# Compressing keys and values with two positions stacked over 128 partitions

## The chip, the cores and the metric

The kernel runs on one core of a Trainium2 chip. The metric is the device time of one execution in microseconds (us). Every time below is either a measured run or comes from one profiled execution.

## The reference

The network is two blocks of two layers each over one sequence of 512 tokens with 1024 channels, in float32. The change touches one step in each of the two layers (l = 0 and 1) of the second block: the compression of keys and values ahead of the sparse attention. Cut to that:

```
CMP_BLOCK = 32; CMP_STRIDE = 16          # two heads (Hkv), hd = 64, T = 512, so 31 blocks

def compress_blocks(k, pe, w1, b1, w2):
    B, T, Hkv, hd = k.shape
    n_cmp = (T - CMP_BLOCK) // CMP_STRIDE + 1
    idx = np.arange(n_cmp)[:, None] * CMP_STRIDE + np.arange(CMP_BLOCK)[None, :]
    blocks = k[:, idx] + pe[None, None, :, None, :]
    flat = jnp.transpose(blocks, (0, 1, 3, 2, 4)).reshape(B, n_cmp, Hkv, CMP_BLOCK * hd)
    return jax.nn.gelu(flat @ w1 + b1, approximate=True) @ w2

    kc = compress_blocks(k_cmp, ck_pe, ck_w1, ck_b1, ck_w2)     # k_cmp = rope(kv[:, :, 0])
    vc = compress_blocks(v_cmp, cv_pe, cv_w1, cv_b1, cv_w2)     # v_cmp = kv[:, :, 1]
    s = jnp.einsum('bthgd,bnhd->bhgtn', qg, kc) * scale         # then softmax, selection, o_cmp
```

A block of 32 positions is two neighbouring groups of 16, so the kernel computes each group's product with both halves of `w1` once and adds shifted columns afterwards.

## The kernel before

Each engine has its own program, written out by hand in order, and waits on semaphores. Activations lie as 128 channels by 512 tokens. TensorE (`tensor_program`) works through projections tile by tile; each tile of eight 128x128 weight pieces is three float32r products per piece (lines 546, 549, 553: high by high, low weights, low activations), 512 columns each. ScalarE makes the high part of each weight piece (`hi_to`, line 1111), VectorE the low part (`lo_to`, line 1562), and both start from a raw copy in `ring`.

SyncE (`sync_program`) issues all weight loads, one unit of up to 512 KB at a time (line 503), into a ring of four slots: unit u waits until unit u - 4 has been used. Between the loads, at unit numbers named in `turns`, it issues the half turns of the rotary embedding (`half_turn`, line 481): four transfers of 32 partitions each within SBUF, which move the rotated halves of piece r into `pp`. Pieces r = 0 (the compressed keys), 1 to 4, 5 and 6 wait for VectorE's scaled projection (`ra`). SyncE's queue is in order, so a transfer waits for all that stand ahead of it. GpSimd multiplies the unturned half (line 2319), VectorE the turned one (2076), and VectorE adds them (2081).

In a layer of the second block TensorE does, in this order: a group of five tiles and the tiles 5, 6 and 7 of `w_in` (the last of them is the last work ahead of compression); the compression (line 976); the projection `tm` by token (lines 623 to 627, 280 columns), with the second small product of compression (`compressed`, lines 990 and 995) hooked in after its fourth piece; the compressed scores (1010); eight tiles `sb`; then attention.

The compression at 976 keeps head 0 in partitions 0 to 63 and head 1 in 64 to 127 of `KC` (keys) and `VCB` (values), each with two groups of 16 columns of position embeddings at the ends. For keys, then values, it runs over two units of `w1` (raw, 1024 columns: 16 positions by 64), and for each position over the two heads: 128 products per layer, each with 64 rows of weights, 64 columns and 32 moving columns. The sum lies in two banks. ScalarE copies the keys' bank (1446), converts three `tm` pieces (1111), and applies the gelu (1451) after VectorE's adds (2105 to 2108); the values' bank follows.

## Time and profile before

| | us |
|---|---|
| three runs, median | 2937.4 |
| lowest and highest | 2935.91 and 2937.46 |
| the profiled execution | 2937.69 |
| its span (first to last instruction) | 2936.0 |

| engine | busy us | share of the span |
|---|---|---|
| TensorE, products (PE) | 2919.7 | 99% |
| TensorE, weight loads (PEld) | 2392.5 | 81% |
| VectorE (DVE) | 1821.4 | 62% |
| ScalarE (ACT) | 1305.0 | 44% |
| GpSimd (POOL) | 155.2 | 5% |

### The profile page before, as it was taken

What the parts mean: (1) busy time and instruction counts of PE and PEld (TensorE: products, weight loads), DVE (VectorE), ACT (ScalarE), POOL (GpSimd) and SP (SyncE); (2) the same over time, 40 slices, a digit from 0 to 9 for tenths busy, and PEclk for the clock granted to TensorE, in tenths of its full rate; (3) what the DMA queues carried; (4) which work ended last, traced back from release to release, by engine and by line L of the source; (5) the groups of instructions that cost most, each with busy time, mean ns of one, the idle gap of its engine ahead of it and who ended that gap; (6) DMA issues with size and microseconds to landing.
All of it is one profiled execution on the core that took longest, in us unless ns stands there. A gap on an engine that the chain in (4) does not pass through costs nothing.

```text
span 2936.0 us, 38238 instructions
## 1 busy us (share of the span) xinstructions
PE 2919.7 (99%) x14742; PEld 2392.5 (81%) x14742; DVE 1821.4 (62%) x3241; ACT 1305.0 (44%) x2458; POOL 155.2 (5%) x204
## 2 busy tenths in 40 slices
PE   9999999999999999999999999999999999999998
PEld 8788888888888888888887688888888877788886
DVE  4666775355555487734666667775365766677743
ACT  4544443233333344432366744443333776444431
POOL 1000000010000000001000101000030011010000
PEclk9999999999999999999999999999999999999999
DMA  4222222222222233333311132222333111323322
GB/s 161 74 101 97 100 97 98 97 87 81 79 78 94 87 101 100 94 101 104 125 51 48 47 108 79 102 94 100 106 113 97 37 51 58 115 72 101 101 93 72
DMA packets 74726, 263.98 MB, mean 90 GB/s; under 512 B 9008, under 2 KB 9008, under 8 KB 74416
## 3 DMA queue, kind: packets, MB, share of 16 engines
q1 hardware_dynamic: 73680, 258.13, 26.3%
q10 hardware_dynamic: 864, 3.41, 0.3%
q8 instruction: 116, 1.90, 0.3%
q14 instruction: 66, 0.54, 0.1%
HBM read 255.74 MB, written 2.10 MB: 88 GB/s over the span
## 4 chain that ended last, share of the span: by engine, by line
PE 96%; DVE 2%; ACT 1%; issue 1%; POOL 0%; DVEq 0%
PE bank L546 27%; PE bank L553 26%; PE bank L549 26%; PE bank L623 2%; PE bank L627 2%; PE bank L624 2%; PE bank L755 2%; PE bank L734 1%; PE bank L719 1%; PE bank L923 1%; PE bank L1029 1%; DVE big L2244 1%; PE bank L1055 1%; ACT big L1541 1%; PE bank L976 1%
## 5 line engine op out<-in xcount | busy, mean ns | idle before, releaser
L1562 DVE TENSOR_TENSOR wl<-ring,wh 128x512 fp32r<-128x512 f32 (+1 forms) x928 | 635.4, 691 | 798.1 <-ACT wh L1111 793.1
L546 PE MATMUL bank<-xh,wh 128*128 128x512 f32 x2392 | 946.0, 395 | 0.1
L549 PE MATMUL bank<-xh,wl 128*128 128x512 f32 x2392 | 932.9, 390 | 0.0
L553 PE MATMUL bank<-xl,wh 128*128 128x512 f32 x2392 | 904.7, 390 | 0.0
L1111 ACT ACTIVATE wh<-ring 128x512 fp32r<-128x512 f32 (+1 forms) x928 | 569.1, 622 | 681.6 <-PE bank L553 606.4
L546 PEld LDWEIGHTS bank<-xh,wh 128*128 128x128 f32 x2392 | 449.6, 188 | 115.9 <-issue 22.2
L553 PEld LDWEIGHTS bank<-xl,wh 128*128 128x128 f32 x2392 | 449.4, 188 | 95.6 <-DVE xl L1682 0.4
L549 PEld LDWEIGHTS bank<-xh,wl 128*128 128x128 f32 x2392 | 449.8, 188 | 89.4 <-DVE wl L1562 1.3
L546 PE MATMUL bank<-bigr,wh 128*128 128x512 f32 x1024 | 398.9, 390 | 0.6 <-ACT bigr L1545 0.6
L549 PE MATMUL bank<-bigr,wl 128*128 128x512 f32 x1024 | 398.4, 389 | 0.0
L553 PE MATMUL bank<-bigr,wh 128*128 128x512 f32 x1024 | 393.4, 389 | 0.0
L546 PEld LDWEIGHTS bank<-bigr,wh 128*128 128x128 f32 x1024 | 192.2, 188 | 41.1 <-ACT bigr L1545 1.5
L553 PEld LDWEIGHTS bank<-bigr,wh 128*128 128x128 f32 x1024 | 192.2, 188 | 40.8 <-DVE bigr L2248 0.9
L549 PEld LDWEIGHTS bank<-bigr,wl 128*128 128x128 f32 x1024 | 192.2, 188 | 39.9
L1315 ACT ACTIVATE tmp<-tmp,vec 128x512 f32<-128x512 f32 x136 | 104.7, 770 | 182.1 <-DVE tmp L1616 182.1
L2273 POOL TENSOR_TENSOR sm<-sm,cst 128x4 f32<-128x4 f32 x16 | 17.7, 1107 | 1931.2 <-DVE sm L1584 1931.2
L1325 ACT ACTIVATE bigr<-tmp 128x512 fp32r<-128x512 f32 x88 | 55.7, 632 | 138.5 <-DVE tmp L1862 138.5
L1186 ACT ACTIVATE pp<-pp,sm 128x512 f32<-128x512 f32 (+3 forms) x160 | 87.9, 551 | 62.0 <-DVE sm L1635 62.0
L623 PE MATMUL bank<-wh,xh 128*128 128x512 f32 (+1 forms) x288 | 106.8, 371 | 0.0
L1616 DVE TENSOR_TENSOR tmp<-bank,rs 128x512 f32<-128x512 f32 x154 | 105.0, 684 | 2.3 <-PE bank L553 1.7
L624 PE MATMUL bank<-wh,xl 128*128 128x512 f32 (+1 forms) x288 | 105.9, 368 | 0.0
L627 PE MATMUL bank<-wl,xh 128*128 128x512 f32 (+1 forms) x288 | 105.7, 367 | 0.0
(258 smaller groups left out, 2976.3 us busy)
## 6 DMA issues: line engine op xcount, KB each, us to landing
ring<-in_w_up SPq DMA_DIRECT2D x176, 512.0 KB, 3.4
ring<-in_w_down SPq DMA_DIRECT2D x88, 512.0 KB, 3.4
ring<-in_w_in SPq DMA_DIRECT2D x64, 512.0 KB, 3.5
ring<-in_w_ret SPq DMA_DIRECT2D x32, 512.0 KB, 3.1
ring<-in_w_even SPq DMA_DIRECT2D x19, 512.0 KB, 3.9
ring<-in_w_ret_v SPq DMA_DIRECT2D x16, 512.0 KB, 3.2
ring<-in_w_ret_out SPq DMA_DIRECT2D x16, 512.0 KB, 3.2
ring<-in_w_proj SPq DMA_DIRECT2D x16, 512.0 KB, 3.4
```

What stands on the lines that cost most here:

```text
L546: e.matmul(o, K.wh(p, c * 128, 128), oh, start=start, stop=False, skip_group_check=True)
L549: e.matmul(o, K.wl(p, c * 128, 128), oh, start=False, stop=False, skip_group_check=True)
L553: m = e.matmul(o, K.wh(p, c * 128, 128), ol, start=False, stop=stop, skip_group_check=True)
L623: e.matmul(o, K.XH[:, c], K.wh(p, 0, n), start=k == 0, stop=False)
L624: e.matmul(o, K.XL[:, c], K.wh(p, 0, n), start=False, stop=False)
L627: m = e.matmul(o, K.XH[:, c], K.wl(p, 0, n), start=False, stop=k == DT - 1)
L755: m = e.matmul(BK[4][u.base:u.base + 64, u.qt * 128:(u.qt + 1) * 128], u.v(kt), K.pt(2 * t + i)[:, c:c + 128], start=u.start and kt == 0, ...
L1111: e.activation(K.wh(i, 0, w), K.raw(i), ACT.Copy, bias=0.0, scale=1.0).then_inc(F.hi.tell(("piece", i)), 1)
L1186: e.activation(p, p, ACT.Exp, bias=K.den(t, 2 * part + i, 0), scale=-1.0, accum_out=K.den(t, 2 * part + i, 1)).then_inc(F.act.tell(("exp", ...
L1315: e.activation(K.tmp((2 * i + 1) % 5), K.up(i), ACT.Identity, bias=b, scale=w[2]).then_inc(F.act.tell(("tap", f, i)), 1)
L1562: e.tensor_tensor(K.wl(i, 0, w), K.raw(i), K.wh(i, 0, w).bitcast(F32), ALU.subtract).then_inc(F.lo.tell(("piece", i)), 1)
L1616: e.tensor_tensor(dst, K.bank(key)[:, :], K.RSB[:, :], ALU.mult).then_inc(F.dve.tell(("freed", *key), *events), 1)
```

## The change

Two new areas, `SK` and `SV`, hold keys and values stacked: partitions 0 to 63 a head's columns as they are, partitions 64 to 127 the same columns shifted by one position; the two heads lie one behind the other (544 columns each). SyncE fills them with eight transfers within SBUF per layer (`vals` after the half turn of piece 2, `keys` after that of piece 4). `w1` is laid out for two positions over 128 partitions, with keys' weights in its first 512 columns and values' in the other 512, which makes two units per layer in place of four. A product now has 128 rows, 64 weight columns and 64 moving columns (32 for each head); keys go to the column half 0 to 63 and values to 64 to 127 of one bank. There are 32 products per layer. The copy, the adds and the gelu handle keys and values together.

```diff
 def weights(D):
-        for i in range(4):
-            W.raw(D[f"w1_{l}"][i], ("w1", l, i))
+        for part in range(2):
+            W.raw(D[f"w1_{l}"][part], ("w1", l, part))
 def sync_program(e, q, K):
+    def stack(l, src, dst, flag, name):
+
+        for kv in range(2):
+            for odd in range(2):
+                e.dma_start(dst[64 * odd:64 * odd + 64, 544 * kv:544 * kv + 544 - odd],
+                            src[64 * kv:64 * kv + 64, odd:544]).then_inc(
+                    flag.tell(*([(name, l)] if kv and odd else []), by=16), 16)
+
+    def keys(l):
+        q.wait_ge(F.dve, ("pe", l))
+        q.wait_ge(F.dve, ("rope", l, 0))
+        stack(l, K.KC, K.SK, F.keys, "keys")
+
+    def vals(l):
+        q.wait_ge(F.dve, ("pe", l))
+        q.wait_ge(F.dve, ("freed", "n", l, "g", 1))
+        stack(l, K.VCB, K.SV, F.vals, "vals")
+
-        turns.update({u + 1: (l, (0, 1)), u + 2: (l, (2,)), u + 3: (l, (3,)), u + 4: (l, (4,)), u + 7: (l, (5, 6))})
+        turns.update({u + 1: (l, (0, 1)), u + 2: (l, (2,)), u + 3: (l, (3,)), u + 4: (l, (4,)), u + 5: (l, (5, 6))})
     for u, (src, width, pieces) in enumerate(W.units):
         if u in turns:
             for r in turns[u][1]:
                 half_turn(turns[u][0], r)
+            if turns[u][1] == (2,):
+                vals(turns[u][0])
+            if turns[u][1] == (4,):
+                keys(turns[u][0])
 def tensor_program(e, q, K):
-            for part in range(2):
-                u = W.raws["w1", l, 2 * i + part]
-                q.wait_ge(K.landed(u), ("unit", u))
-                for n in range(16):
-                    for kv in range(2):
-                        r = slice(64 * kv, 64 * kv + 64)
-                        m = e.matmul(BK[b][r, 32 * part:32 * part + 32], K.slot(u)[r, n * 64:(n + 1) * 64],
-                                     c[r, 2 * part:2 * part + 32, n], start=part == 0 and n == 0, stop=n == 15,
-                                     skip_group_check=True)
-                m.then_inc(F.attn.tell(("cmp", l, i, part), ("unit", u)), 1)
-            vacated[b] = [(F.act, ("hb", l, i))]
+        b = K.place["cb", l] = spare[0]
+        q.wait_ge(F.vals, ("vals", l))
+        q.wait_ge(F.keys, ("keys", l))
+        empty(b)
+        for part in range(2):
+            u = W.raws["w1", l, part]
+            q.wait_ge(K.landed(u), ("unit", u))
+            for n in range(8):
+                for i, c in enumerate((K.skr, K.svr)):
+                    at_w = 512 * i + 64 * n
+                    m = e.matmul(BK[b][64 * i:64 * i + 64, 64 * part:64 * part + 64], K.slot(u)[:, at_w:at_w + 64],
+                                 c[:, :, 2 * part:2 * part + 32, 2 * n], start=part == 0 and n == 0, stop=n == 7,
+                                 skip_group_check=True)
+            m.then_inc(F.attn.tell(("cmp", l, part), ("unit", u)), 1)
 def scalar_program(e, q, K):
-        for i in range(2):
-            q.wait_ge(F.attn, ("cmp", l, i, 1))
-            e.activation(K.hb(i), K.bank(("cb", l, i))[:, 0:64], ACT.Copy, bias=0.0, scale=1.0).then_inc(
-                F.act.tell(("hb", l, i)), 1)
-            if i == 0:
-                hi_to(W.first["tm", l] + 2)
-            q.wait_ge(F.dve, ("hid", l, i))
+        q.wait_ge(F.attn, ("cmp", l, 1))
+        e.activation(K.hb, K.bank(("cb", l))[:, 0:128], ACT.Copy, bias=0.0, scale=1.0).then_inc(F.act.tell(("hb", l)), 1)
+        hi_to(W.first["tm", l] + 2)
+        q.wait_ge(F.dve, ("hid", l))
+        e.activation(bc(K.hid[:, 64:128], [[32, 2], [1, 31]]), bc(K.hid, [[32, 2], [1, 31]]), ACT.Gelu_apprx_tanh,
+                     bias=K.SM[:, 160:161], scale=1.0).then_inc(F.act.tell(("gel", l)), 1)
```

SyncE's queue in layer 0, from the first unit of `w1` to the first of `sb`. Before (`ring<-in_w_0` is a unit of `w1`, `pp<-tmp` a half turn, x8 is two of them):

```order
L503 DMA ring<-in_w_0 128x1024
L481 DMA pp<-tmp 32x512 x8
L503 DMA ring<-in_w_0 128x1024
L481 DMA pp<-tmp 32x512 x4
L503 DMA ring<-in_w_0 128x1024
L481 DMA pp<-tmp 32x512 x4
L503 DMA ring<-in_w_0 128x1024
L481 DMA pp<-tmp 32x512 x4
L503 DMA ring<-in_w_tm 128x840 x2
L503 DMA ring<-in_w_tm 128x560
L481 DMA pp<-tmp 32x512 x8
```

After:

```order
L524 DMA ring<-in_w_0 128x1024
L480 DMA pp<-tmp 32x512 x4
L487 DMA big<-big 64x544
L487 DMA big<-big 64x543
L487 DMA big<-big 64x544
L487 DMA big<-big 64x543
L524 DMA ring<-in_w_tm 128x840
L480 DMA pp<-tmp 32x512 x4
L524 DMA ring<-in_w_tm 128x840
L480 DMA pp<-tmp 32x512 x4
L487 DMA big<-big 64x544
```

The first four `big<-big` are the values', and the keys' four begin in the last row shown, behind the half turn of piece 4; the loads between them are `tm` where `w1` stood.

TensorE around the compression of layer 0. Before:

```order
L549 MATMUL bank<-xh,wl 128x512
L553 MATMUL bank<-xl,wh 128x512
L976 MATMUL bank<-big,ring 64x32 x128
L623 MATMUL bank<-wh,xh 128x280
L624 MATMUL bank<-wh,xl 128x280
```

The last two rows are the first `tm` products. After:

```order
L570 MATMUL bank<-xh,wl 128x512
L574 MATMUL bank<-xl,wh 128x512
L992 MATMUL bank<-big,ring 64x64 x32
L644 MATMUL bank<-wh,xh 128x280
L645 MATMUL bank<-wh,xl 128x280
```

The 128 products have become 32, and the neighbours are the same. ScalarE at that place (`wh<-ring 128x280` are the `tm` pieces). Before:

```order
L1443 ACT_TABLE_LOAD
L1446 ACTIVATE big<-bank 128x64
L1111 ACTIVATE wh<-ring 128x280 x3
L1451 ACTIVATE big<-big,sm 128x31
L1446 ACTIVATE big<-bank 128x64
L1451 ACTIVATE big<-big,sm 128x31
```

Each 128x64 copy takes one bank, each 128x31 gelu one of keys and values. After:

```order
L1457 ACT_TABLE_LOAD
L1459 ACTIVATE big<-bank 128x128
L1125 ACTIVATE wh<-ring 128x280 x3
L1462 ACTIVATE big<-big,sm 128x2x31
L1125 ACTIVATE wh<-ring 128x280 x4
```

The first copy waited for half of the compression (keys) and now waits for all of it; the three `tm` pieces stand behind it both times.

## Rows read from the trace of the kernel before

**Rows 1.** Busy time, granted clock and DMA share by stretch (busy us and count per engine)

```profile
1385.00:1393.30 8.30, 8.30 (x38) 6.63 (x36) 5.44 (x9) 0.00 (x0) 3.35 (x3) 1.00 0.88 240
1393.30:1401.00 7.70, 7.70 (x258) 7.61 (x257) 4.63 (x8) 1.31 (x4) 2.87 (x2) 1.00 0.62 185
```

**Rows 2.** Timeline of TensorE at both compressions (start us, extent us)

```profile
1393.35 7.66 PE L976 MATMUL bank<-big,ring 64*64 64x32 f32 x256
1400.94 0.40 PE L623 MATMUL bank<-wh,xh 128*128 128x280 f32 x1
...
2182.60 7.66 PE L976 MATMUL bank<-big,ring 64*64 64x32 f32 x256
2190.19 0.40 PE L623 MATMUL bank<-wh,xh 128*128 128x280 f32 x1
```

**Rows 3.** Timeline of TensorE: other column halves, full arrays, the second small product

```profile
1407.27 0.30 PE L990 MATMUL bank<-big,vec 64*64 64x31 f32 x2
1407.50 0.30 PE L995 MATMUL bank<-vec,big 64*31 64x64 f32 x4
...
1408.19 0.40 PE L623 MATMUL bank<-wh,xh 128*128 128x280 f32 x1
...
1414.45 3.76 PE L1010 MATMUL bank<-big 128*128 128x64 f32 x32
1418.01 0.47 PE L546 MATMUL bank<-xh,wh 128*128 128x512 f32 x1
...
1497.33 1.97 PE L755 MATMUL bank<-pp,big 128*64 128x128 f32 x32
1499.23 0.39 PE L719 MATMUL bank<-tmpr 64*128 64x256 f32 x2
```

**Rows 4.** Weight loads of line 995: timeline row, then durations of its source line

```profile
1407.49 0.14 PEld L995 LDWEIGHTS bank<-vec,big 64*31 64x31 f32 x4
...
L995 PEld LDWEIGHTS bank<-vec,big x16: 102/104/105, 1407.5 to 2197.2; 64*31 64x31 f32 x16
```

**Rows 5.** Timeline of SyncE's DMA issues in both layers, and one lone load

```profile
1384.72 2.41 SPq L481 DMA_DIRECT2D pp<-tmp  x4
1387.29 0.46 SPq L503 DMA_DIRECT2D ring<-in_w  x1
...
1390.87 2.41 SPq L481 DMA_DIRECT2D pp<-tmp  x4
1395.45 4.06 SPq L503 DMA_DIRECT2D ring<-in_w_tm  x3
...
56.39 0.33 SPq L503 DMA_DIRECT2D ring<-in_sel  x1
...
2167.77 4.95 SPq L481 DMA_DIRECT2D pp<-tmp  x8
```

**Rows 6.** Timeline of GpSimd: the product that waits for piece 4's half turn

```profile
1396.09 1.28 POOL L2319 TENSOR_TENSOR tmp<-tmp,rope 128x512 f32<-128x512 f32 x1 [1.20 <-DMA pp<-tmp]
...
2185.43 1.71 POOL L2319 TENSOR_TENSOR tmp<-tmp,rope 128x512 f32<-128x512 f32 x1 [3.56 <-DMA pp<-tmp]
```

**Rows 7.** Timeline of VectorE: keys' rotary sum, tile 7's last low part, `tm`

```profile
1384.63 0.69 DVE L2081 TENSOR_TENSOR big<-tmp,pp 128x512 f32<-128x512 f32 x1 [1.25 <-POOL tmp L2319]
1385.24 0.68 DVE L1562 TENSOR_TENSOR wl<-ring,wh 128x512 fp32r<-128x512 f32 x1
...
1399.76 1.17 DVE L1562 TENSOR_TENSOR wl<-ring,wh 128x280 fp32r<-128x280 f32 x3 [1.84 <-ACT wh L1111]
```

**Rows 8.** Timeline of ScalarE: the copy of the bank and the `tm` pieces

```profile
1397.32 0.22 ACT L1446 ACTIVATE big<-bank 128x64 f32<-128x64 f32 x1 [12.81 <-PE bank L976]
1399.29 1.09 ACT L1111 ACTIVATE wh<-ring 128x280 fp32r<-128x280 f32 x3 [1.75 <-DMA ring<-in_w_tm]
```

**Rows 9.** The one fall of the clock: stretches, then TensorE's timeline around it

```profile
30.00:34.10 4.10, 4.03 (x31) 3.47 (x30) 2.88 (x6) 2.97 (x5) 0.00 (x0) 1.00 0.00 0
34.10:37.50 3.40, 3.40 (x10) 2.62 (x9) 0.26 (x1) 0.00 (x0) 0.00 (x0) 0.50 0.42 154
...
30.77 2.84 PE L679 MATMUL bank<-cst,tmp 128*128 128x2 f32 x24
...
35.64 0.63 PE L546 MATMUL bank<-xh,wh 128*128 128x512 f32 x1
36.07 0.63 PE L549 MATMUL bank<-xh,wl 128*128 128x512 f32 x1
...
38.60 0.39 PE L546 MATMUL bank<-xh,wh 128*128 128x512 f32 x1
38.83 0.39 PE L549 MATMUL bank<-xh,wl 128*128 128x512 f32 x1
```

More of the change, by code:

```diff
@@ L45 @@
 FLAGS = ("proj", "stat", "attn", "hi", "act", "lo", "dve", "pool", "land0", "land1", "land2", "land3",
-         "rot0", "rot1", "rot2", "rot3", "rot4", "warm", "x0", "first", "x1", "x2", "x3", "x4", "gain", "cst", "vec", "pos", "dil", "ret", "out")
+         "rot0", "rot1", "rot2", "rot3", "rot4", "keys", "vals", "warm", "x0", "first", "x1", "x2", "x3", "x4", "gain", "cst", "vec", "pos", "dil", "ret", "out")
 class Flag:
@@ L349, in memory @@
     K.at_ropes = [0, S, 2 * S, 3 * S, 2048, 2560]
-    K.hid, K.gates = K.big(20640, 128), K.big(20896, 96)
+    K.SK, K.SV = K.big(11424, 1088), K.big(12512, 1088)
+    K.skr, K.svr = (t.rearrange("p (v n r) -> p v n r", v=2, r=16) for t in (K.SK, K.SV))
+    K.hid, K.hb, K.gates = K.big(20640, 128), K.big(20768, 128), K.big(20896, 96)
     K.gv = K.gates.rearrange("p (q n) -> p q n", q=NQ)
@@ L982, in compressed @@
+        vacated[b] = [(F.act, ("hb", l))]
         def compressed():
             w2 = K.VC[:, VEC["w2"] + 128 * l:VEC["w2"] + 128 * l + 128]
+            q.wait_ge(F.act, ("gel", l))
+            empty(4)
             for kv in range(2):
-                r = slice(64 * kv, 64 * kv + 64)
-                q.wait_ge(F.act, ("gel", l, 0))
-                if kv == 0:
-                    empty(4)
-                e.matmul(BK[4][r, 0:31], w2[r, 0:64], K.hid[r, 64:95], start=True, stop=True,
-                         skip_group_check=True).then_inc(F.attn.tell(("kc", l, kv)), 1)
@@ L992, in compressed @@
-                q.wait_ge(F.act, ("gel", l, 1))
+                e.matmul(BK[4][64 * kv:64 * kv + 64, 0:31], w2[0:64, 0:64], K.hid[0:64, 64 + 32 * kv:95 + 32 * kv], start=True,
+                         stop=True, skip_group_check=True).then_inc(F.attn.tell(("kc", l, kv)), 1)
+            for kv in range(2):
                 empty(5 + kv)
                 for c in (32 * kv, 64 + 32 * kv):
-                    m = e.matmul(BK[5 + kv][c:c + 31, 0:64], K.hid[r, 96:127], w2[r, 64:128], start=True, stop=True,
+                    m = e.matmul(BK[5 + kv][c:c + 31, 0:64], K.hid[64:128, 64 + 32 * kv:95 + 32 * kv], w2[64:128, 64:128], start=True, stop=True,
@@ L2101, in vector_program @@
         rope(4)
[L2102 to L2109 removed]
+        hb, bias = K.hb, K.SM[:, 160:161]
+        q.wait_ge(F.act, ("hb", l))
+        e.tensor_tensor(bias, hb[:, 0:1], hb[:, 95:96], ALU.add).then_inc(F.dve.tell(("hbias", l)), 1)
+        e.tensor_tensor(bc(K.hid, [[32, 2], [1, 31]]), bc(hb[:, 1:128], [[32, 2], [1, 31]]), bc(hb[:, 64:128], [[32, 2], [1, 31]]),
+                        ALU.add)
+        q.wait_ge(F.dve, ("hbias", l))
+        e.tensor_tensor(bias, bias, K.vec("b1", l), ALU.add).then_inc(F.dve.tell(("hid", l)), 1)
         e.memset(K.kcc, 0.0)
@@ L2443 @@
         put("conv_b_2", columns(a["conv_b_2"][l]), 44 * l)
+        put("b1", np.concatenate([a["ck_b1_2"][l], a["cv_b1_2"][l]])[:, None], l)
         for i, c in enumerate(("k", "v")):
-            put("b1", np.tile(a[f"c{c}_b1_2"][l], 2)[:, None], 2 * l + i)
             put("pe", np.tile(a[f"c{c}_pe_2"][l].T, (2, 1)), 64 * l + 32 * i)
```

30 lines of the change are left out of this document (3 added, 27 removed).

## The prediction

> **What bounds the kernel now.** I read the table of engines and the chain that ended last first: TensorE is busy for 99% of the span and carries 96% of the chain, so what shortens or delays TensorE by a microsecond moves the end by about that. The stages then show the place. In the 8.3 us ahead of the compression and in the 7.7 us of it TensorE is never idle and the clock is 1.00 [rows 1]. The compression takes 7.59 us in each layer, from its first record at 1393.35 to the next line's at 1400.94, and from 2182.60 to 2190.19 [rows 2]: 256 records, so 29.6 ns each. All the change can save is inside these 15.2 us, and it saves only if the operands are there when TensorE arrives, since nothing else is left between tile 7 and the compression that it could do.
>
> **The new products.** 32 float32 products are 64 records per layer. At the pace of line 976 they take 64 x 29.6 ns = 1.9 us, with about 0.2 us for the last to finish 2.1 us. Two things differ. They stream 64 columns, not 32, and their two tiles share all 128 rows and differ only in the column half. The nearest row with such tiles is line 755: 32 records of 128 rows by 64 columns with 128 moving columns, keys' and values' halves in turn, in 1499.23 - 1497.33 = 1.90 us, 59.4 ns each [rows 3]. Half the columns at that pace per column is 29.7 ns. If the time were that of the loads and not of the columns it would stay 59.4 ns, 3.8 us in all. Line 995, with the same rows and other column groups, has its four weight loads done within 0.14 us, while one takes 0.102 to 0.105 [rows 4], so loads into different column groups run side by side. I take 1.9 us and keep 3.8 us as the upper bound.
>
> The rule that speaks against the change stands in the Trainium skill, "TensorE: Matmul & The Clock Gate", Part 3 (The mechanism): a weight load overlaps a running product only where the row group differs. Line 976 had two row groups, the new products have one. By that rule each record would cost load and product one after the other. The loads of line 995 do not look like it.
>
> **The transfers, and when TensorE may start.** SyncE's queue is in order, and the keys' four transfers stand behind the half turn of piece 4 and behind the values' four. The order of that queue is otherwise unchanged: a load, four transfers, a load, four transfers. Neither the loads that now are `tm` nor their slots make SyncE wait longer: their predecessors in the ring are the units of tiles 6 and 7 (and of tile 5 for the second unit of `w1`), whose conversions end with the low part at 1385.24 [rows 7]. So the time at which the keys have landed is the time at which piece 4's half turn lands now, plus eight transfers.
> - Piece 4's turn: GpSimd's product that waits for it starts at 1396.09 in layer 0 and 2185.43 in layer 1, released by the DMA both times [rows 6].
> - One transfer within SBUF costs SyncE 4.95 / 8 = 0.62 us, and 0.63 us from start to start where four stand in a row [rows 5]. The new ones have 64 partitions of 2.1 KB and not 32 of 2 KB. A lone load of 128 partitions costs 0.33 us to issue [rows 5], so the partitions alone don't set the price. I take 0.63 us, since these are the same kind of transfer, one behind the other in the same queue; the bounds are 0.33 us and twice 0.63. Eight are 5.0 us (2.6 to 10.1).
> - The keys' rotary sum, for which they also wait, is done at 1385.3 [rows 7] and sets nothing.
>
> TensorE can start at 1396.09 + 5.0 = 1401.1 and at 2185.43 + 5.0 = 2190.4. It arrives at 1393.35 and 2182.60. **It waits 7.8 us in each layer**, more than the compression took. Queued behind this wait on TensorE is all the rest of the layer; ScalarE, VectorE and SyncE in turn wait for its products. The DMAs carry about as much as before (1.1 MB more within SBUF, 1.05 MB less of weights, per layer), though they were busy for 88% of the stretch ahead [rows 1], which speaks for the upper side.
>
> **What stands behind the last product.** Before, ScalarE's copy waited for the keys' half only, and the `tm` pieces were converted at 1399.29, while TensorE still compressed values [rows 8]; line 623 followed at once. Now the copy waits for all, and the first piece stands behind it: copy 0.22 us, first piece 1.09 / 3 and some fixed time, about 0.44 us, and a signal each way of about 0.05: TensorE waits some 0.75 us. VectorE's low part of the piece (1.17 us for three, the first about 0.45 us [rows 7]) starts then, while TensorE has 0.36 us of work without it: 0.15 us more. Together 0.9 us (0.75 to 1.2). From the start of compression to `tm` it is 2.1 + 0.9 = 3.0 us.
>
> **The clock.** The clock fell once in this trace: in 30.00 to 34.10 TensorE had 24 records of 2 moving columns for 2.8 us, and in 34.10 to 37.50 it was granted 0.50 (1.2 GHz, otherwise 2.4). There products of 512 columns start 0.43 us apart and not 0.23 us [rows 9], so 3.4 us of it cost 1.6 us. A wait of 7.8 us is a good deal emptier than that, and I expect a fall in each layer, with the first microseconds after the wait at the lower level. How much of the low stretch falls on work is not to be read before; 1.6 us is the price of one such stretch all filled with work, twice that is my upper bound, zero the lower one. I take 2.2 us. The Trainium skill has the same in "TensorE: Matmul & The Clock Gate", Part 1: an idle engine is throttled to half, and activity releases it.
>
> **The second small product.** Lines 990 and 995 alternate twice and take 1408.19 - 1407.27 = 0.92 us, 0.23 us for each of four changes of shape [rows 3]. Now there are two groups with the same products; I take 0.6 us, a gain of 0.3 us (0 to 0.5). Their operands pass through ScalarE and VectorE in fewer steps (one copy, one gelu, three adds per layer), and the hook comes four `tm` pieces after the start, so nothing waits there. The later half turns (5 and 6) and the `sb` loads follow the compression by as much as before, 13 us or so ahead of their use (line 546 at 1418.01 [rows 3]): no cost.
>
> **The sum per layer:** wait 7.8 + compression up to `tm` 3.0 + clock 2.2 - second product 0.3 - what it was 7.6 = **+5.1 us**. Two layers: +10.2 us. The profiled execution took 2937.69 us, 0.3 above the median, so I put it on the median: 2937.4 + 10.2 = 2947.6 us.
>
> **Rivals.**
> 1. *The transfers are there in time, and the kernel is faster.* The mechanism would be SyncE reaching the keys' transfers before TensorE reaches the compression, with only 3.0 - 0.3 - 7.6 = -4.9 us per layer left: 2927.6 us. It decides at a wait of 4.9 us: keys landed by 1398.25. For it speaks that their data are ready at 1385.3. Against it the queue: piece 4's half turn is issued at 1390.87 to 1393.28 even now [rows 5], and both sets of transfers come on top. At 0.33 us each they land at 1398.7, and even then with a fall of the clock it is a loss. 5%.
> 2. *Cheap transfers, or no fall of the clock.* With 0.33 us each and 1.6 us for the clock the sum is 7.8 - 2.4 + 3.0 + 1.6 - 0.3 - 7.6 = +2.1 us per layer, 2941.6 us; with 0.63 us and no fall +2.9, 2943.2 us. Both count as no change or just not. 15%.
> 3. *Dear transfers.* If the price goes by partitions, 1.26 us each, the keys land 5 us later still: +10.1 us per layer, 2957.6 us. For it speaks that twice as many rows move per transfer and that the DMAs are near full; against it that 128 partitions are issued in 0.33 us. 10%.
> 4. *Column halves that don't load side by side.* With load and product in a row as on a full array, where line 1010 takes (1418.01 - 1414.45) / 32 = 111 ns per record [rows 3], 64 records are 7.1 us: +10.3 us per layer, 2958.0 us. At 59.4 ns it is +7.0, 2951.4 us, which is within the forecast's range. The Trainium skill's rule on row groups, named above, asks for the first. 5% for it, since rows 4 speak against.
>
> **How the numbers follow.** Forecast 2947.6 us, 65%, its own range 2943.3 to 2955 (transfers of 0.5 to 0.9 us, clock 1.6 to 3.2, pace up to 59 ns). The range for 8 in 10 takes in most of rival 2 and the near part of 3: 2941.5 to 2957.5 us. About 0.2% (5.9 us) is what a measurement of this kernel can tell from no change. Faster by more than that: rival 1, 5%. Within it: rival 2 mostly and a little of rival 1, 13%. Slower: 82%.
>
> **What would show it.** In the changed kernel's profile TensorE should sit idle ahead of the compression for 7 to 8 us, released by the DMA into the stacked area and not by VectorE; the eight transfers should stand 0.63 us apart in SyncE's row; the 64 records should be paced near 30 ns at full clock, or near 60 at half, with the granted clock at 0.50 after the wait; about 0.75 us idle before the first `tm` product, released by ScalarE. If the wait is under 5 us, or TensorE finds the keys landed, the step on SyncE's queue is wrong. If the compression itself takes 4 us or more at the full clock, the step on column halves is.

## The result, and the profile of the changed kernel

The changed kernel takes 2944.4 us (median of 10 runs, 2942.7 to 2945.4), against 2936.0 us (10 runs, 2935.7 to 2937.9) for the kernel before, measured beside it. The ratio is 1.0026 (95% interval 1.0016 to 1.0035). The forecast was 2947.6 us, in a range of 2941.5 to 2957.5. The profiled execution took 2944.9 us, with a span of 2943.2 us; before, the span was 2936.0 us.

Executions differ by up to 2.0 us in when TensorE gets to the first compression. So a second number helps where profiles are compared: the time from TensorE's arrival at the first compression to the end of the span. Before it is 2936.0 - 1393.35 = 1542.65 us, after it is 2943.2 - 1393.28 = 1549.92 us, 7.3 us more. Below this is called the **rest time**. (The arrival is 0.32 us after the start of the last product of tile 7, which is where the first product of the compression starts if nothing holds it, as in e5 below.)

TensorE's timeline at both compressions (start us, extent us, line, shapes, count, then idle time ahead and who ended it), to be read beside [rows 2] and [rows 3]:

```profile
1392.96 0.39 PE L574 MATMUL bank<-xl,wh 128*128 128x512 f32 x1
...
1400.43 3.85 PE L992 MATMUL bank<-big,ring 128*64 128x64 f32 x64 [7.08 <-issue]
1404.98 0.40 PE L644 MATMUL bank<-wh,xh 128*128 128x280 f32 x1 [0.69 <-ACT wh L1125]
...
1411.54 0.30 PE L1004 MATMUL bank<-big,vec 64*64 64x31 f32 x4
1411.77 0.32 PE L1009 MATMUL bank<-vec,big 64*31 64x64 f32 x8
1412.02 0.40 PE L644 MATMUL bank<-wh,xh 128*128 128x280 f32 x1
...
2193.39 3.90 PE L992 MATMUL bank<-big,ring 128*64 128x64 f32 x64 [6.88 <-issue]
2197.98 0.52 PE L644 MATMUL bank<-wh,xh 128*128 128x280 f32 x1 [0.69 <-ACT wh L1125]
```

From the arrival at 1393.28 to the first `tm` product at 1404.98 it is 11.7 us, where [rows 2] had 7.6. Three pieces make them up: 7.15 us of waiting, 3.85 us of products, 0.70 us of hand-off. The second small product takes 1412.02 - 1411.54 = 0.48 us, where [rows 3] had 0.92. The profile names "issue" as what ended the long wait, that is nothing it could match. SyncE's queue says what it was (the first four rows are its timeline, to be read beside [rows 5]; the last two are what the trace holds on the transfers' line):

```profile
1387.27 2.51 SPq L487 DMA_DIRECT2D big<-big  x4
1389.94 0.47 SPq L524 DMA_DIRECT2D ring<-in_w_tm  x1
...
1393.57 2.41 SPq L480 DMA_DIRECT2D pp<-tmp  x4
1396.02 2.52 SPq L487 DMA_DIRECT2D big<-big  x4
...
L487 SPq DMA_DIRECT2D big<-big x16: 592/597/606, 1387.3 to 2191.0; - x16
...
DMA to landing us min/median/max: 2.3/2.4/2.8
```

The keys' last transfer is issued at 1397.93 and lands 2.41 us later, at 1400.34. TensorE's first product starts at 1400.43.

The stretches around the wait in layer 0 (busy us and count of PE, PEld, DVE, ACT, POOL, then granted clock, DMA share, GB/s), to be read beside [rows 1]:

```profile
1396.10:1400.40 4.30, 0.00 (x0) 0.00 (x0) 1.99 (x3) 0.00 (x0) 1.79 (x2) 0.50 0.77 176
1400.40:1402.90 2.50, 2.47 (x44) 2.50 (x46) 0.00 (x0) 0.00 (x0) 0.00 (x0) 0.50 0.00 0
1402.90:1404.30 1.40, 1.39 (x26) 1.15 (x22) 0.00 (x0) 0.00 (x0) 0.00 (x0) 0.98 0.50 133
...
1405.00:1412.00 7.00, 7.00 (x60) 6.54 (x60) 5.14 (x14) 2.46 (x7) 2.58 (x2) 1.00 0.56 148
```

The clock does fall to 0.50 (1.2 GHz), but in layer 0 it is back ahead of `tm`. And the products hardly notice it: taken from start to start, the 64 records are 57 ns apart in the stretch at 0.50 and 56 ns in the one behind it. In layer 1 all of them run at 0.50 and are 57 ns apart. (Extent by count gives 60 ns, since the extent holds some 0.3 us for the last record to finish. Below, a pace is always the mean from start to start of the trace's single records, which the rows here show only in sum; for [rows 2] that is 29.2 ns. The records come in pairs: the second starts 3 to 40 ns behind the first, and the next pair 112 to 114 ns behind this one.)

### The profile page after: what moved, and what is told of

Same layout as the page of the kernel before. It is cut to its first block, busy times and chain, and to the rows that moved or that the text cites. A ratio compares the mean times of both kernels' runs of the same rounds, so it can differ in the third digit from the quotient of the medians.

```text
span 2943.2 us, 37473 instructions
## 1 busy us (share of the span) xinstructions
PE 2912.0 (99%) x14358; PEld 2384.6 (81%) x14358; DVE 1820.4 (62%) x3235; ACT 1304.1 (44%) x2454; POOL 155.4 (5%) x204
## 4 chain that ended last, share of the span: by engine, by line
PE 95%; DVE 2%; ACT 1%; issue 1%; POOL 0%; DVEq 0%
PE bank L567 26%; PE bank L570 26%; PE bank L574 26%; PE bank L644 2%; PE bank L648 2%; PE bank L645 2%; PE bank L776 2%; PE bank L755 1%; PE bank L740 1%; PE bank L944 1%; PE bank L1043 1%; DVE big L2254 1%; PE bank L1069 1%; ACT big L1552 1%; PE bank L930 1%
```

## The experiments

Two questions are left by this profile. Is it really the place of the transfers in SyncE's queue that costs 7 us? And why are the records 56 to 57 ns apart, at either clock, and not 30?

**e1: the transfers on ScalarE's queue.** ScalarE has nothing to do between projection 7's weight pieces and the bank copy.

```
 def scalar_program:
+        vals(l)
+        keys(l)
         e.preload_act_table_set("gelu_apprx_tanh_and_others")
         q.wait_ge(F.attn, ("cmp", l, 1))
 def sync_program:
-            if turns[u][1] == (2,):
-                vals(turns[u][0])
-            if turns[u][1] == (4,):
-                keys(turns[u][0])
```

> The changed kernel, with its eight transfers per layer issued by ScalarE (idle from 1384.4 to 1404.3 us in layer 0) and no longer by SyncE. Theory on the wait (they stand behind SyncE's half turns): ScalarE can issue them from 1383.2 on, at 0.63 us each they are out by 1388.3 and landed by about 1391, so TensorE's wait of 7.15 us is gone and the clock stays at 1.00. Rival (the DMA engines, not the queue, are the limit): they land little earlier than in the changed kernel and the wait stays above 4 us. Two theories on the 55 to 57 ns per record that the changed kernel's compression shows: (A) half clock, column halves run side by side, then it is 29.6 ns here, compression 2.1 us, and the kernel takes 2926 us; (B) the weight loads of tiles that share their rows are serial, then it stays 53 to 57 ns at full clock, compression 3.6 us, and the kernel takes 2929 us.

**e2: the same, and `tm`'s first high pieces ahead of the bank copy.**

```
+        hi_to(W.first["tm", l] + 2)
         q.wait_ge(F.attn, ("cmp", l, 1))
         e.activation(K.hb, K.bank(("cb", l))[:, 0:128], ...)
-        hi_to(W.first["tm", l] + 2)
         q.wait_ge(F.dve, ("hid", l))
```

> As the run before, and ScalarE converts the three tm pieces ahead of its copy of the bank, not behind it. Theory (the 0.7 us idle before the first tm product is the copy and the first piece in a row, and 0.1 us for the low part): 0.7 to 0.85 us less per layer, 1.5 us in all, first tm product right behind the last of compression. Rival (tm not landed or its slot not free at that time, since the slot is vacated by tile 7): the idle stays.

Measured: e1 2937.8 us (2934.0 to 2942.5, 11 runs), ratio to the kernel before 1.0003 (0.9994 to 1.0012). e2 2936.9 us (2933.8 to 2942.3, 11 runs), ratio 1.0001 (0.9992 to 1.0010). The kernel before stood at 2937.3 beside both. TensorE's timeline in e1, layer 0, then the one row of layer 1 at the compression:

```profile
1391.58 3.79 PE L970 MATMUL bank<-big,ring 128*64 128x64 f32 x64
1396.06 0.40 PE L622 MATMUL bank<-wh,xh 128*128 128x280 f32 x1 [0.69 <-ACT wh L1103]
...
1400.32 0.40 PE L626 MATMUL bank<-wl,xh 128*128 128x280 f32 x1 [3.74 <-DVE wl L1571]
...
2184.61 3.83 PE L970 MATMUL bank<-big,ring 128*64 128x64 f32 x64 [1.74 <-issue]
```

The wait of 7 us is gone in layer 0 and down to 1.7 us in layer 1. So it was SyncE's queue. But in layer 0 most of the gain goes into the next wait: `tm`'s low part, 3.74 us, since VectorE's order has it inside its fifth rotary step, behind the half turns. The granted clock falls behind this wait too, and here the low stretch is filled with `tm`:

```profile
1400.70:1404.10 3.40, 3.40 (x17) 3.40 (x16) 2.99 (x10) 1.11 (x3) 1.29 (x1) 0.50 0.76 229
```

From the first `tm` product to the first one of `sb` it is 22.2 us in e1 and 16.9 us in e4 (below), where nothing waits and the clock stays up: 3.7 us more of waiting and 1.6 us more for the same work at the lower clock. In layer 1 the low parts cost 0.7 us. VectorE in e1, at an earlier of the rotary steps:

```profile
1390.91 0.69 DVE L2085 TENSOR_TENSOR pp<-pp,rope 128x512 f32<-128x512 f32 x1 [3.52 <-DMA pp<-tmp]
```

It waits 3.52 us for a half turn, and all behind it in its order comes later. Two queues now issue at once, and transfers take longer to land. In e2 the landings in 1376 to 1400 us show it (transfers, KB each, median us from issue to landing):

```profile
pp<-tmp SPq DMA_DIRECT2D x26, 64.0 KB, 2.8
...
big<-big ACTq DMA_DIRECT2D x4, 136.0 KB, 4.1
big<-big ACTq DMA_DIRECT2D x4, 135.8 KB, 5.4
```

On SyncE's queue alone the same transfers landed in 2.4 us. In layer 1 (2168 to 2192 us) it shows in the half turns as well:

```profile
pp<-tmp SPq DMA_DIRECT2D x24, 64.0 KB, 4.2
...
big<-big ACTq DMA_DIRECT2D x4, 136.0 KB, 5.5
big<-big ACTq DMA_DIRECT2D x4, 135.8 KB, 6.9
```

In the changed kernel the half turns there took 2.5 us. In e2 the keys come 1.1 and 3.8 us too late. The idle 0.69 us ahead of `tm` is gone in both its layers, as expected, but the 1.5 us that this was to bring over e1 are not shown: the medians are 0.9 us apart, and the ranges overlap. The record's pace in e1 also settles a point: 56 ns at a clock of 1.00 with no wait ahead (layer 0). The half clock is not its cause.

**e3: no transfers for the values.** The value products read the stacked keys, so the values' compression is left out.

```
             if turns[u][1] == (2,):
-                vals(turns[u][0])
...
-        q.wait_ge(F.vals, ("vals", l))
...
-                for i, c in enumerate((K.skr, K.svr)):
+                for i, c in enumerate((K.skr, K.skr)):
```

> The changed kernel without the values' four transfers and the wait for them; the values' products read the stacked keys, so the values' result is left out. Queue theory: the keys are issued 2.5 us earlier, the wait falls from 7.15 to 4.6 us in each layer, 5 us in all. Rival (landing is set by the bytes that the DMA engines have in hand or by the keys' own transfers): the wait falls by less than 1 us.

Measured: 2938.6 us (one run), rest time 1545.3 us, 4.6 less than the changed kernel's. The waits are 4.9 us in both layers, now with their releaser named:

```profile
1396.59 3.79 PE L989 MATMUL bank<-big,ring 128*64 128x64 f32 x64 [4.92 <-DMA big<-big]
...
2187.37 3.87 PE L989 MATMUL bank<-big,ring 128*64 128x64 f32 x64 [4.84 <-DMA big<-big]
```

Four transfers fewer take 2.2 and 2.0 us off the waits, where they take 2.5 us to issue and 2.5 were expected. The rival said less than 1 us. So issue time in the queue is the main part of the wait, at 0.5 us for each transfer by this run.

**e4: TensorE kept warm in the wait** by 30 products of 512 columns on a bank that nobody reads.

```
+        keep(30, b)
         q.wait_ge(F.vals, ("vals", l))
         q.wait_ge(F.keys, ("keys", l))
```

> The changed kernel with 30 products of a constant tile (6.8 us) in the wait, so that the clock does not fall; the wait's end is the same. (A) half clock was the cause of the slow compression: it takes 2.1 us here and the kernel 4 us less than the changed one. (B) serial loads: 3.5 to 3.7 us here, the kernel at most 1 us less.

Measured: 2942.9 us (one run). The granted clock stays at 1.00, and the compression takes the same 3.8 us:

```profile
1391.53 6.97 PE L662 MATMUL bank<-warm 128*128 128x512 f32 x30
1399.02 3.79 PE L993 MATMUL bank<-big,ring 128*64 128x64 f32 x64 [0.51 <-issue]
```

The rest time is 2941.1 - 1391.63 = 1549.5 us (the arrival again 0.32 us after the start of tile 7's last product), 0.4 us less than the changed kernel's. The waits differ a little too (7.4 and 6.8 us here). Without them, the compressions are 0.06 and 0.07 us shorter than in the changed kernel, and `tm` with what follows up to `sb` 0.00 and 0.19 us. So the fall of the clock costs 0.3 us in the changed kernel's two layers.

Up to here my explanation of the 56 ns was that two tiles which share rows load their weights one after the other. Three kernels, all with e1's queue, were made to test it.

**e6: one head.** Half the moving columns; the second head is left out of the compression.

```
-                    m = e.matmul(BK[b][64 * i:64 * i + 64, 64 * part:64 * part + 64], ...,
-                                 c[:, :, 2 * part:2 * part + 32, 2 * n], ...)
+                    m = e.matmul(BK[b][64 * i:64 * i + 64, 64 * part:64 * part + 32], ...,
+                                 c[:, 0, 2 * part:2 * part + 32, 2 * n], ...)
```

> The kernel of e1 with 32 moving columns per product in place of 64: the second head is left out of the compression. Theory B (the weight load of 128 rows x 64 columns sets the pace, and loads of tiles that share rows come one after the other): the 64 records of a layer still take 3.8 us, 55 to 59 ns each. Rival A (load and product alternate without overlap, 27 + 27 ns at full clock): the product halves, about 42 ns a record, 2.7 us a layer. Rival C (columns alone): 28 ns, 1.9 us.

**e7: tiles of 64 rows.** Each product is split into two; the odd positions' half goes to a second bank and is left out of the sum.

```
+                for odd in range(2):
                     for i, c in enumerate((K.skr, K.svr)):
+                        r = slice(64 * (i ^ odd), 64 * (i ^ odd) + 64)
-                    m = e.matmul(BK[b][...], K.slot(u)[:, at_w:at_w + 64], c[:, :, 2 * part:2 * part + 32, 2 * n], ...)
+                        m = e.matmul(BK[(b, b2)[odd]][...], K.slot(u)[r, at_w:at_w + 64], c[r, :, 2 * part:2 * part + 32, 2 * n], ...)
```

> The kernel of e1 with each 128-row product of the compression split into two of 64 rows, one on the same row half and one on the other, the odd positions' into a second bank that is not added in (so half of each sum is left out): neighbours now share neither rows nor columns. 128 records a layer in place of 64. Theory B (sharing rows is what makes the loads serial): 29.6 ns a record as in the kernel before, 3.8 us a layer in all, no gain and no loss. Rival (a pace of 55 ns belongs to any record of 64 x 64 with this order of operands): 7.1 us a layer, and the span 6.6 us longer than e1's.

**e8: the column halves apart.** All keys' products of a unit, then all values'.

```
-            for n in range(8):
-                for i, c in enumerate((K.skr, K.svr)):
+            for i, c in enumerate((K.skr, K.svr)):
+                for n in range(8):
```

> The kernel of e1 with the eight products of the keys ahead of the eight of the values in each unit, so that neighbours lie in the same column half but for one change per unit. Theory B (loads alone set the pace, and each load overlaps the product before it, whichever half that is in): the same 3.8 us a layer. Rival (a load overlaps a product only if it goes to the other column half, so alternating is what keeps the pace at 55 ns): load and product in turn, 80 to 111 ns a record, 5.1 to 7.1 us a layer.

TensorE's row for the compression of layer 0, in e6, e7 and e8:

```profile
1393.18 2.07 PE L970 MATMUL bank<-big,ring 128*64 128x32 f32 x64
```

```profile
1391.89 3.85 PE L974 MATMUL bank<-big,ring 64*64 64x64 f32 x128 [0.33 <-issue]
```

```profile
1393.75 5.99 PE L970 MATMUL bank<-big,ring 128*64 128x64 f32 x64 [0.52 <-issue]
```

(One run each: 2941.4, 2939.5 and 2938.2 us. The places behind the compression differ as in e1, so only the compressions are compared. All three ran that of layer 0 at a clock of 1.00.)

- e6: records **29 ns apart**, with the same loads as e1, where they are 56 ns apart. If loads in a row had set the 56 ns, they would be there still. My theory falls, and rival C's 28 ns holds. What halved is the columns, so the moving columns set the pace.
- e8: 90 ns apart in the mean, inside its rival's 80 to 111. The single records say more. Where neighbours lie in the same column half they start 110 ns apart; only around the three changes of half do they start in pairs, as in e1. And in e1 each half gets a record every 112 ns, two of them in turn every 56. So **a column half keeps its pace whether or not the other one works beside it**; e1 has both at work, e8 mostly one.
- e7: 28 ns apart, as expected, but for another reason (neighbours share a row half at every second step, which the expectation overlooked). Four tiles are in turn, and each gets a record of 64 columns every 112 ns, which is the pace of a half in e1.

The counts of records in 1 us show the difference between one half and two, first e8 (x12), then e1 (x23; both counts hold some that started up to 0.3 us ahead of the window):

```profile
1394.00:1395.00 1.00, 1.00 (x12) 1.00 (x11) 0.00 (x0) 0.00 (x0) 1.00 (x1) 1.00 1.08 266
```

```profile
1392.00:1393.00 1.00, 1.00 (x23) 1.00 (x20) 0.16 (x1) 0.00 (x0) 0.74 (x1) 1.00 1.07 315
```

The rival's reason for e8's pace was that load and product follow one another in the same half. That isn't shown, and rows of the kernel before speak against it. On the full array a record with 2 moving columns takes 112 ns (line 679 in [rows 9], from start to start), and one with 128 columns 109 ns:

```profile
1493.66 1.91 PE L734 MATMUL bank<-cst,pp 128*128 128x128 f32 x16
```

If load and product took turns there, 126 more columns would cost something. I read these rows so: each column half is a tile that works by itself, its loads are hidden behind its products, and 64 moving columns of this kind take it 110 ns. No run was made to test this reading against others.

Of the Trainium skill the page "TensorE: Matmul & The Clock Gate", Part 3 (The mechanism), says that a load overlaps a running product only where the row group differs. On the full array all records have the same row groups, and yet 126 more moving columns add nothing to a record (109 ns against 112), so its load isn't added to its product; here the measurement decides against the rule. Nor does the rule name the column half, and with the same row groups in both, the records are 56 ns apart in e1 and 110 within a half in e8.

**e5: stacking by ScalarE.** A copy of 64 partitions may write into the other 64, so ScalarE can do what the eight transfers did. `tm`'s high pieces stand ahead of the bank copy, and VectorE's low parts ahead of its fifth rotary step.

```
 def stack(l, src, dst, name):
-                e.dma_start(dst[64 * odd:64 * odd + 64, 544 * kv:544 * kv + 544 - odd],
-                            src[64 * kv:64 * kv + 64, odd:544]).then_inc(...)
+                m = e.activation(dst[64 * odd:64 * odd + 64, 544 * kv:544 * kv + 544 - odd],
+                                 src[64 * kv:64 * kv + 64, odd:544], ACT.Copy, bias=0.0, scale=1.0)
+        m.then_inc(F.act.tell((name, l)), 1)
...
         e.preload_act_table_set("gelu_apprx_tanh_and_others")
+        vals(l)
+        keys(l)
+        hi_to(W.first["tm", l] + 2)
         q.wait_ge(F.attn, ("cmp", l, 1))
...
-        hi_to(W.first["tm", l] + 2)
...
-            if r == 4:
-                lo_to(W.first["tm", l] + 2)
...
+        lo_to(W.first["tm", l] + 2)
         rope(4)
```

> All eight transfers per layer become eight copies of 64 partitions x 543 or 544 columns on ScalarE (same partitions or the other half), behind its last weight piece of the projections; tm's first high pieces stand ahead of the bank copy, and VectorE's low parts of them ahead of its wait for piece 4's half turn. Theory (the wait was issue time and landing behind the half turns, not the stacking itself): copies at about 0.65 us each are done 5.2 us after the table load at 1383.2 to 1384.4, so by about 1390, ahead of TensorE's arrival at 1391.6 to 1393.3; no wait ahead of the compression, 3.8 us of products, tm behind it with no idle time, the second small product at 0.5 us. Against the kernel before that is 7.6 - 3.8 = 3.8, plus 0.44 from the second product, so some 8.5 us in the two layers: about 2928 us against 2937. Rival: something else ends at the same time (tm's low parts on VectorE behind a half turn, or tm's weights not landed): a wait of 1 to 3 us moves ahead of tm, and the time is 2930 to 2935. Second rival: the copies write the other half of the partitions slowly or crowd ScalarE out of tm's pieces: a wait on ScalarE ahead of the compression or ahead of tm, time at or above 2935.

Measured: 2929.0 us (2927.3 to 2930.5, 7 runs) against 2937.5, **ratio 0.9970 (0.9959 to 0.9981)**. TensorE in layer 0, then ScalarE's copies:

```profile
1392.92 0.39 PE L552 MATMUL bank<-xl,wh 128*128 128x512 f32 x1
1393.24 3.85 PE L969 MATMUL bank<-big,ring 128*64 128x64 f32 x64
1397.02 0.40 PE L622 MATMUL bank<-wh,xh 128*128 128x280 f32 x1
...
1384.41 5.36 ACT L1433 ACTIVATE big<-big 64x544 f32<-64x544 f32 x8
```

The copies are done at 1389.8, 3.5 us ahead of TensorE. No wait is left ahead of the products or of `tm`; one of 0.58 us stands inside `tm` in layer 0. The rest time is 2928.6 - 1393.24 = 1535.4 us, 7.3 less than before's (8.6 by the medians). So the stacked compression, with the `tm` pieces moved ahead, is worth 7 to 9 us if its data come in time, and costs 7 to 8 if they come through SyncE's queue.

**e9, e10: the step of the moving columns.** The products read positions 16 elements apart. e9 has ScalarE write only the positions that are read, in the order in which they are read; e10 is e5 with adjacent columns read in place of the right ones, which leaves the compression's values out.

```
e9:
-                m = e.activation(dst[64 * odd:64 * odd + 64, 544 * kv:544 * kv + 544 - odd],
-                                 src[64 * kv:64 * kv + 64, odd:544], ACT.Copy, ...)
+                m = e.activation(bc(dst[64 * odd:64 * odd + 64, 272 * kv:], [[34, 8], [1, 34]]),
+                                 bc(src[64 * kv:64 * kv + 64, odd:], [[2, 8], [16, 34]]), ACT.Copy, ...)
-                                 c[:, :, 2 * part:2 * part + 32, 2 * n], ...)
+                                 bc(c[:, 34 * n + 2 * part:], [[272, 2], [1, 32]]), ...)
e10:
-                                 c[:, :, 2 * part:2 * part + 32, 2 * n], ...)
+                                 bc(c[:, 34 * n + 2 * part:], [[544, 2], [1, 32]]), ...)
```

> The kernel of e5, but ScalarE's eight copies leave out the positions that no product of that half reads and store the others in the order in which the products read them: 64 x 272 columns each, and a product's two runs of 32 moving columns lie side by side instead of 64 bytes apart. e6 showed that 32 moving columns take 32 ns a record and 64 take 59, so the moving columns set the pace, at about 1.2 a ns, at full clock here and at the half clock in the changed kernel alike. Theory S (the 64-byte step of the moving operand is what holds it to 1.2 columns a ns): the 64 records of a layer fall from 3.8 us to the load's pace, 30 to 36 ns each, 2.0 to 2.3 us, and the time by 3 to 3.6 us against e5, to about 2925.5. Theory F (a record of an fp32 product takes its columns at 1.2 a ns, whatever the step): 3.8 us as before, time as e5's, 2929. Under both the copies fall from 5.4 us to 3 to 4 us, off the path.

> The kernel of e5 with one change: the products of the compression read 2 x 32 columns that lie side by side in the stacked tiles instead of 64 bytes apart; these are not the positions that belong to the sum, so the compression's values are left out. Theory S (step): 2.0 to 2.3 us for the 64 records of a layer, and a span 3 to 3.6 us under e5's 2928.6. Theory F (fp32 rate): 3.8 us, and e5's span.

Measured: e9 2928.1 us (2925.9 to 2930.0, 6 runs), ratio 0.9969 (0.9957 to 0.9981); e10 2929.3 us (one run). TensorE in e9, layer 0 (two rows and the next wait), and ScalarE's copies; then e10's compression:

```profile
1393.01 2.08 PE L969 MATMUL bank<-big,ring 128*64 128x64 f32 x64
...
1397.11 0.40 PE L626 MATMUL bank<-wl,xh 128*128 128x280 f32 x1 [1.56 <-DVE wl L1570]
...
1384.18 5.59 ACT L1433 ACTIVATE big<-big 64x272 f32<-64x272 f32 x8
```

```profile
1393.47 2.08 PE L969 MATMUL bank<-big,ring 128*64 128x64 f32 x64
```

3.85 us fall to 2.08, 56 ns a record to 29. e10 differs from e5 in nothing but which columns are read and the step between them, so **it was the 64-byte step of the moving operand**. (e6 reached 29 ns at the same step with half the columns: 32 with the step cost what 64 adjacent ones do.) The Trainium skill has this rule in "SBUF — State Buffer", section "Door 1: The DMA port swizzle": each read that crosses to a new 16-byte line pays, so fp32 may step by up to 4 elements for nothing. The step here is 16, and the runs agree that it costs; no run has a step between 1 and 16. Of the 1.8 us a layer about half arrives: TensorE now waits 1.56 and 0.92 us for `tm`'s low parts, and the rest time is 1533.3 us, 2.1 less than e5's, where 3 to 3.6 were expected. By the medians it is 0.8 us, and the ranges overlap. The expectation missed the copies too: half the elements take as long as all of them (5.59 against 5.36 us), so copies that read with this step cost twice as much per element.

**e11: the low parts one place earlier.**

```
         times_rs(K.tmp(0), ("n", l, 6), s, ("ra", l, 5))
+        lo_to(W.first["tm", l] + 2)
         rope(3)
         ...
-        lo_to(W.first["tm", l] + 2)
         rope(4)
```

> The kernel of e9 with VectorE's low parts of tm's first three pieces one place earlier, ahead of its wait for piece 3's half turn and of projection 7's eviction (e9: its low parts began at 1396.2 to 1396.8, TensorE waited 1.56 and 0.92 us for them). Theory (the low parts' place is all that ends last there): the wait is gone, -2.5 us against e9, about 2925.6. Rival: the three low parts push back projection 7's eviction and piece 3's rotary sum by 2 us and something behind them waits instead: e9's time, 2928, or more.

Measured: 2926.6 us (2925.0 to 2927.3, 5 runs), ratio to the kernel before 0.9960 (0.9947 to 0.9974). TensorE's waits behind the compression:

```profile
1399.41 0.39 PE L626 MATMUL bank<-wl,xh 128*128 128x280 f32 x1 [0.43 <-DVE wl L1570]
...
2183.89 0.40 PE L622 MATMUL bank<-wh,xh 128*128 128x280 f32 x1 [1.30 <-ACT wh L1102]
```

The waits for the first low parts are gone (2.5 us), and others of 1.7 us stand a little later, in the part that ends with gelu. The rest time is 1533.0 us, e9's was 1533.3. The profiled execution of e11 is 1.6 us shorter than e9's, but TensorE reaches its compression 1.3 us earlier: the clock did not fall at 34 us in it, as it did in e9's and in the kernel before's [rows 9]. So the median's 1.5 us under e9 isn't borne out by the profiles, and the two runs' ranges overlap. The expected gain of 2.5 us over e9 is not shown; that the kernel beats the one before by 0.3 to 0.5% is.

**e12: adjacent columns in the changed kernel,** with its transfers and its wait (the compression's values are left out, as in e10). The edit is e10's.

> The changed kernel, transfers and wait and all, but with the moving columns side by side in place of 64 bytes apart (other positions are read, so the compression's values are left out). TensorE's granted clock will have fallen to 0.50 in the wait, as in the changed kernel. If the half clock alone also holds a record to 1.2 columns a ns, the 64 records of layer 1, all at 0.50, take 3.4 to 3.8 us as in the changed kernel, and those of layer 0 that lie behind the clock's return fall to 32 ns each; then step and clock are two caps of one size, and the fall cost nothing only because the step already held the pace. If the granted clock doesn't touch these records at all, both layers take 2.1 us and the time is 3.4 us under the changed kernel's 2944.4.

Measured: 2948.7 us (one run), rest time 1553.6 us. TensorE in layer 0, its compression in layer 1, and the stretches behind the wait there:

```profile
1400.28 3.68 PE L992 MATMUL bank<-big,ring 128*64 128x64 f32 x64 [6.93 <-issue]
1404.65 0.60 PE L644 MATMUL bank<-wh,xh 128*128 128x280 f32 x1 [0.69 <-ACT wh L1125]
...
2195.59 3.68 PE L992 MATMUL bank<-big,ring 128*64 128x64 f32 x64 [7.45 <-issue]
...
2197.00:2200.00 3.00, 2.31 (x44) 2.12 (x41) 0.06 (x1) 0.70 (x3) 0.00 (x0) 0.50 0.41 120
2200.00:2202.00 2.00, 2.00 (x8) 2.00 (x9) 2.00 (x8) 0.55 (x2) 0.02 (x1) 0.50 0.52 131
...
2204.00:2205.00 1.00, 1.00 (x7) 1.00 (x6) 0.10 (x1) 0.00 (x0) 0.00 (x0) 0.57 0.49 117
```

With adjacent columns at the half clock the records are 53 ns apart, where at the full clock they are 29. So the step and the half clock each hold the pace to 1.1 or 1.2 columns a ns, and they don't add up (57 ns with both). That is why the changed kernel's products took the same time at both levels. Second, the clock came back only at about 2204.9 here, in the middle of `tm`, 13.7 us after its fall, and in layer 0 it stayed down for 13.7 us as well; in the changed kernel it was 6.8 us both times. From the first `tm` product to `sb` it is 18.9 us in both layers, 2.0 us more than in e4, which had the full clock. That is near the 2.2 us that the prediction had put on the fall. (The rest time is 3.7 us longer than the changed kernel's; the waits and the products differ too, by 0.4 us in sum each, with opposite signs.) Why the clock came back later than in the changed kernel stays open: the waits were shorter in one layer (6.93 against 7.08 us) and longer in the other (7.45 against 6.88), and the products took about the same time.

## Why the prediction was right

The result (+8.4 us by the medians measured side by side, 2944.4 in all, where +10.2 and 2947.6 were forecast) lies within the forecast's own range, and the main reason stood: TensorE waits for transfers in SyncE's queue for about as long as the compression took. But two terms were off by 1.75 and about 2 us a layer in opposite directions. That they nearly cancel was luck, and the sum is better than its parts.

- **The wait: right.** 7.8 us forecast, 7.15 and 6.95 measured. The issue of 0.63 us for each of eight transfers held: from the end of piece 4's turn before (1393.28) to the end of the keys' issue now (1398.54) it is 5.3 us, where 5.0 were forecast, and e3 confirms the place by taking four away. What was 0.9 us too much is the landing: I had taken GpSimd's start behind piece 4's half turn, 2.8 us behind the end of that turn's issue [rows 5, 6], and the keys' transfers took 1.9 us from the end of issue to the first product (1398.54 to 1400.43).
- **The products: too cheap by 1.75 us a layer.** "Half the columns at that pace per column is 29.7 ns" is the sentence that failed. The pace per column of line 755 [rows 3] holds for adjacent columns (e10: 29 ns); these stand 64 bytes apart, and cost 56 to 57. I kept 3.8 us as the upper bound, for a different reason, loads in a row; e6 shows that this isn't the reason. The step was in the diff and in the code of before, and no term of the sum looked at it.
- **The clock: too dear by about 2 us a layer.** It fell in both layers, as forecast. But the low stretch of 1396.1 to 1403.0 covered 4.3 us of waiting and 2.5 us of products that the step held to nearly the same pace. What was left is the first 0.3 us of `tm`, in layer 1. e4 puts the whole at 0.3 us. That it could have been 2 us a layer shows in e12.
- **The hand-off: right.** 0.9 us forecast, 0.92 measured: 0.70 up to the first `tm` product, and the 0.2 us for the low part. The fourth `tm` product starts 0.71 us behind the first one now (1405.69), and 0.49 before.
- **The second small product: right in sign.** 0.3 us forecast, 0.44 us measured; both were within the bounds.
- **The sum.** 7.15 + 3.85 + 0.92 - 0.44 - 7.6 = +3.9 us in layer 0, and the same is measured from TensorE's arrival to the first `sb` product (1421.85 after, 1418.01 before). Two layers make 7.8 us; behind layer 1's `sb` the changed kernel is 0.6 us faster, which nothing in the forecast names, and the rest times differ by 7.3.

Of the rivals, the first (keys in time) never came near: the wait was 7 us, and it decides at 4.9. e5 reaches 2929.0 us where that rival had said 2927.6. But e5 has no hand-off, which that sum still held at 0.9 us, and its products take 1.75 us more, so its nearness is in part luck again; that only SyncE's queue stood against the rival is borne out. The second (cheap clock) was half right: the clock cost almost nothing, though it did fall. The fourth had the right size at 59.4 ns and the wrong mechanism. Its other size, 111 ns of line 1010, is not load and product in a row either: records with 2 columns come as far apart on the full array [rows 9].

## What to carry to other kernels

When work moves onto transfers, count what stands ahead of them in the issuing queue and price it by issue time: eight small transfers, set among the rotary turns of one queue, brought a wait of 7 us a layer, while an idle engine's copies of the same data brought none. Price a product by the step of its moving operand as well as by its columns; a record of 64 columns costs 29 ns with adjacent columns and 56 with columns 64 bytes apart. And when a wait is taken away, look for the next one in the other engines' order before the gain is booked: in e1's layer 0, 5.3 of the 7 us went to a low part that stood behind somebody else's wait, and to the lower clock that followed.

## What the runs showed of the hardware

- An fp32 record of 128 rows by 64 columns and 64 moving columns, with the two column halves in turn, takes 29 ns at the full clock with adjacent columns and 56 ns with a 64-byte step; at the half clock it takes 53 and 57 ns (e10, e1, e12, the changed kernel).
- A column half gets such a record with the step every 110 to 112 ns, whether the other half has work in between (e1) or not (e8, where neighbours lie in the same half). Two halves double the pace, though both use all rows.
- On the full array a record takes 112 ns with 2 moving columns and 109 ns with 128 (lines 679 and 734 of the kernel before), so its load is not added to its product.
- Line 976 in [rows 2] had the 64-byte step as well: two tiles in turn, each with a record of 32 columns every 58 ns. A half of e6, with 32 such columns, has the same 58 ns.
- Transfers within SBUF that landed in 2.4 us from SyncE's queue took 4.1 and 5.4 us (medians of four) from ScalarE's while SyncE was issuing too, and 5.5 and 6.9 us in layer 1, where the half turns came in 4.2 us in place of 2.5 (e2).
- ScalarE copies 64 partitions into the other 64, 0.66 us for 544 fp32 elements, and takes 0.69 us for 272 that it reads with a step of 64 bytes (e5, e9).
- The clock came back 6.8 us after its fall in both layers of the changed kernel and 13.7 us after it in both layers of e12, with waits of 6.9 to 7.5 us.
